# A two-layer decoder step on one core: rows of a retention head turned inside the next head's second projection, partial sums copied first, products for the new state two steps earlier

## The reference

```
proj = h @ w_ret_in                      # per head: q and k (256 + 256), v (512), g (512)
scores = (q_i @ k_i.T) * decay_mat       # chunks of 128 rows
o = scores @ v_i + (q_i * q_decay) @ s
s = chunk_decay * s + (k_i * k_decay).T @ v_i
y = layernorm(o) * gn * silu(g)          # rows of one head, 512 wide
x = x + gate * (y @ w_ret_out)
```

## Time and profile before

| what | value |
|---|---|
| median of 3 runs (lowest, highest) | 657.1 us (657.0 to 658.63) |
| the profiled execution, its own time | 656.73 us |
| its span, first to last instruction | 654.9 us |
| TensorE busy | 607.1 us (93% of the span) |
| VectorE, ScalarE, GpSimd busy | 363.6, 237.2, 214.5 us |
| TensorE's mean granted clock | 0.984 |
| the four heads, first projection of head 0 to the end of head 3 | about 37 to 297 us |
| moved by DMA | 190.30 MB |

### The profile page before, as it was taken

The page is one execution under the profiler, slowest core; times in us unless marked ns, Lnnn a source line. Parts: engine busy times, 40 slices in busy tenths (PEclk is TensorE's granted clock), DMA queues, the critical chain, the costliest instruction groups (busy, mean ns, idle before and its releaser), DMA issues. The chain is left out here.

```text
span 654.9 us, 11425 instructions
## 1 busy us (share of the span) xinstructions
PE 607.1 (93%) x4335; PEld 378.9 (58%) x4335; DVE 363.6 (56%) x726; ACT 237.2 (36%) x488; POOL 214.5 (33%) x242
## 2 busy tenths in 40 slices
PE   6899999899989998998999999999999988659996
PEld 5576656666666666743567746777644555434441
DVE  3343747375736583646544723445797964873822
ACT  4245244524442444223223625554044246231010
POOL 0060128012702270204283368999800012110000
PEclk9999999999999999998999999999999999788998
DMA  8996374897589658993995734544999999999982
GB/s 306 378 384 250 130 272 156 304 357 259 171 311 356 238 202 295 376 389 127 318 336 205 259 134 144 187 176 155 385 397 397 409 406 407 408 400 410 400 346 84
DMA packets 82370, 190.30 MB, mean 291 GB/s; under 512 B 4167, under 2 KB 12631, under 8 KB 82316
## 3 DMA queue, kind: packets, MB, share of 16 engines
q1 hardware_dynamic: 80484, 183.71, 75.5%
q0 software_dynamic: 1296, 4.46, 2.4%
q10 hardware_dynamic: 536, 1.41, 0.6%
HBM read 167.14 MB, written 22.41 MB: 289 GB/s over the span
## 5 line engine op out<-in xcount | busy, mean ns | idle before, releaser
L553 POOL TENSOR_TENSOR weights_low<-ring,weights_high 128x512 fp32r<-128x512 f32 x96 | 124.0, 1332 | 74.3 <-PE bank L800 39.9
L1391 ACT ACTIVATE weights_high<-ring 128x1024 fp32r<-128x1024 f32 x84 | 86.6, 1054 | 101.1 <-PE bank L819 55.7
L811 PE MATMUL bank<-weights_high,h_high 128*128 128x512 f32 x272 | 109.2, 402 | 0.0
L811 PE MATMUL bank<-weights_high,h_low 128*128 128x512 f32 x272 | 107.1, 394 | 0.0
L819 PE MATMUL bank<-weights_low,h_high 128*128 128x512 f32 x272 | 83.9, 404 | 4.7 <-DVE weights_low L553 4.5
L811 PEld LDWEIGHTS bank<-weights_high,h_high 128*128 128x128 f32 x272 | 51.0, 188 | 25.5 <-issue 14.2
L819 PEld LDWEIGHTS bank<-weights_low,h_high 128*128 128x128 f32 x272 | 48.9, 188 | 20.8 <-DVE weights_low L553 7.5
L811 PEld LDWEIGHTS bank<-weights_high,h_low 128*128 128x128 f32 x272 | 51.2, 188 | 11.0
L553 DVE TENSOR_TENSOR weights_low<-ring,weights_high 128x512 fp32r<-128x512 f32 x72 | 44.7, 684 | 16.6 <-PE bank L710 11.4
L1975 DVE SCALAR_TENSOR_TENSOR ring<-ring,bank 128x512 f32<-128x512 f32 x64 | 41.8, 684 | 18.4 <-PE bank L994 14.9
L1915 DVE TENSOR_TENSOR partial_low<-bank,partial_high 128x512 fp32r<-128x512 f32 x26 | 17.8, 686 | 56.9 <-ACT partial_high L1342 31.0
(11 more groups left out here) (272 smaller groups left out, 1008.6 us busy)
## 6 DMA issues: line engine op xcount, KB each, us to landing
ring<-in_w_ada SPq DMA_DIRECT2D x12, 2048.0 KB, 13.4
ring<-in_cache_k SPq DMA_DIRECT2D x40, 512.0 KB, 8.6
ring<-in_cache_v SPq DMA_DIRECT2D x40, 512.0 KB, 9.9
ring<-in_w_ret_in SPq DMA_DIRECT2D x8, 2048.0 KB, 12.6
ring<-in_state_ret SPq DMA_DIRECT2D x32, 512.0 KB, 9.2
out_state_sample<-ring SPq DMA_DIRECT2D x32, 512.0 KB, 6.9
ring<-in_w_moba_in SPq DMA_DIRECT2D x8, 2048.0 KB, 8.9
arena<-in_cache_k SPq DMA_DIRECT2D x24, 512.0 KB, 10.8
```

Of the source, the lines that this page charges most:

```text
L553: tensor_tensor(w_low[:, slot, k, :], ring[:, slot, k * CH:(k + 1) * CH], high[:, k, :].bitcast(F32), ALU.subtract).then_inc(low_ready[LOW ...
L811: pe.matmul(o[i][:, :], xs[p][i][:, k, :], high[:, k, :], start=k == 0 and p == 0, stop=False)
L1391: nc.scalar.activation(w_high[u[0] == "moba"][:, 2 * i:2 * i + 2, :].rearrange("p a b -> p (a b)"), w[:, 2 * i * CH:(2 * i + 2) * CH], ACT ...
```

## The change

1. TensorE: the new-state products of the head before are called at k = 0, 2, 4, 6 of unit 0 in place of 2, 4, 6, 8.
2. TensorE: the y tiles of the head before are turned one at a time at k = 2, 4, 6 of unit 1, no longer all three after it.
3. ScalarE: `copy_part` of unit 0 stands ahead of all roundings of unit 1's weights; `copy_part` of unit 1 stands ahead of all roundings of unit 2's weights (this holds in head 0 too); the copies of turned tiles 0 and 1 stand ahead of the first two of these roundings, that of tile 2 between the two pairs.

The rows of the last head are still turned after the loop, all three together. No instruction is added or left out, and no DMA.

```
-            def turn_y(h):
-                for n in range(3):
+            def turn_y(h, tiles=(0, 1, 2)):
+                for n in tiles:
                     pe.wait_ge(y_ready, 3 * h + n + 1)
                     turn(("yT", h, n), [L0["y"][:, n, k * P:(k + 1) * P] for k in range(4)])
...
-                if k in (2, 4, 6, 8):
-                    new_four(h - 1, k // 2 - 1)
+                if k < KT and k % 2 == 0:
+                    new_four(h - 1, k // 2)
+
+            def y_of_head_before(k):
+
+                if k in (2, 4, 6):
+                    turn_y(h - 1, (k // 2 - 1,))
...
-                project_parts(("ret", h, 1), ("ret", h, 1))
-                if h:
-                    turn_y(h - 1)
+                project_parts(("ret", h, 1), ("ret", h, 1), y_of_head_before if h else None)
...
-                high_weights(("ret", h, 1), range(2))
                 copy_part(("ret", h, 0))
-                high_weights(("ret", h, 1), range(2, 4))
+                high_weights(("ret", h, 1), range(4))
...
+                copy_part(("ret", h, 1))
+
+                def y_turned(tiles):
+                    if h:
+                        for n in tiles:
+                            turned(L0["yT"][:, 4 * h - 4:4 * h, :], ("yT", h - 1, n), n)
+
+                y_turned((0, 1))
                 high_weights(("ret", h, 2), range(2))
-                copy_part(("ret", h, 1))
+                y_turned((2,))
                 high_weights(("ret", h, 2), range(2, 4))
-                if h:
-                    for n in range(3):
-                        turned(L0["yT"][:, 4 * h - 4:4 * h, :], ("yT", h - 1, n), n)
```

## The result

| | before | changed |
|---|---|---|
| median (lowest, highest), 4 runs each | 657.51 us (657.0 to 658.63) | 650.58 us (649.46 to 651.73) |
| ratio of the two, 95% interval | | 0.9892 [0.9867, 0.9918] |
| profiled execution, its span | 654.9 us | 648.0 us |
| TensorE's mean granted clock | 0.984 | 0.984 |

The changed kernel is 1.1% faster. The forecast was 650.4 us, a gain of 6.7; the measured gain is 6.9, and its interval goes from 5.4 to 8.7.

The account below looks back on a forecast made before the run. The prediction took TensorE, working 93% of the span, as the bound. Terms 6.2 + 1.65 - 1.1 = 6.7 us took the profiled 656.73 us to 650.0; the median, 0.37 above, gave 650.4 us, range 648.2 to 654.2.

Parts of the forecast that it names:

- What TensorE gains in the heads reaches the end: TensorE's gain in the heads should move layer 1's cache stage and the end; 1.3 us either way behind the heads.
- the sum: Gains of 6.2 and 1.65 us in units 1, less 1.1 us lost in units 0: 6.7 us.
- Partial sums copied first: Unit 1, all four heads: copying ahead of the roundings removes TensorE's wait for weight slice 6, 6.2 us gained.
- rival (d): Unit 1: slice 6 waits for something other than ScalarE's copy; 656.6 us, chance 0.04.
- Turned rows inside: Heads 1 to 3: transposes of y inside unit 1 shorten the section behind it; 0.55 us a head, 1.65 us gained.
- rival (c): Unit 1: transposes between matmuls don't overlap, each takes some 0.28 us, costing 6.1 us; 656.5 us, chance 0.03.
- Products two steps earlier: Unit 0, heads 1 to 3: waits for banks of 0.9 us in place of 0.55; some 1.1 us lost.
- The earlier writes and loads: In each head SyncE writes states and issues weight and modulation loads about 2 us earlier; no gain counted.
- rival (a): Head 3: DMAs don't come forward with TensorE; third modulation load follows its slot, 1.8 us return as wait; 652.2 us, chance 0.12.
- a sign of being wrong: Head 3 waiting for modulation weights or states by more than 0.2 us was one of those listed.
- Rival (b), the clock: After new short waits or at late stops the granted clock goes wrong: 1.3 to 3 us lost; 652.5 us, chance 0.09.
- Rival (e), the products tie TensorE to VectorE: Unit 0: every product set waits for VectorE's reads, over 4 us lost a head; 660.7 us at 3.4 more; chance 0.04.

Follow-up runs that it names:

- e1: The kernel before with only ScalarE's two copies of partial sums put first, ahead of the weight roundings: 652.03 us, ratio 0.9911.
- e3: The changed kernel with the new-state products back at k = 2, 4, 6, 8: 650.28 us, ratio 0.9878 to the kernel before.
- e2: The changed kernel with the partial-sum copies behind two roundings again and the products back in their place, leaving only the turns moved: 652.28 us, ratio 0.9912.
- e5: The changed kernel itself, run again beside other variants on one chip: 650.16 us, ratio 0.9891 to the kernel before.
- e6: The changed kernel with VectorE's two prompt-state copies ahead of the third layer norm in heads 0 to 2: 650.58 us, ratio 0.9886.
- e8: e3 with half of each odd new state of head 2 left unwritten, so that output is incomplete: 648.98 us, ratio 0.9861.
- e10: The changed kernel itself, run again in the last group of runs: 650.57 us, ratio 0.9893 to the kernel before.
- e11: The changed kernel with products at k = 1, 3, 5, 7 and VectorE's prompt-state copies ahead of the third layer norm: 649.79 us, ratio 0.9886.
- e9: The changed kernel with the new-state products at k = 1, 3, 5, 7: 649.02 us, ratio 0.9874 to the kernel before.

## Why the prediction held, step by step

- *What TensorE gains in the heads reaches the end.* 6.24 us in the heads' record, 6.9 in the span and in the medians. Right. That the medians meet the forecast to 0.2 us is luck: the heads gave 0.5 us less than the sum, and the rest of the 6.9 lies in stretches that vary by more than that in recordings of one kernel. In the changed kernel units 1 with their turns gave 8.0 us where the sum has 7.85, units 0 took 1.97 where it has 1.1, and head 3's rest gave 0.19.
- *Partial sums copied first, 6.2 us.* Alone it gave 0.63 us in head 0 and 1.94, 2.00, 1.52 in the others, 6.1 us in units 1 (e1). Right, and rival (d) with it out.
- *Turned rows inside, 1.65 us.* The changed kernel's stages with late products (e3) are 0.70 us shorter than e1's, 2.1 us for three: 0.45 us better than the sum. The section behind the unit takes 2.04 us in them and not head 0's 2.10, as its wait for VectorE is 0.44 us and not 0.51, and the three sets add 1.24 us (1.29 in the changed kernel) and not 1.32. A set costs 0.44 us in its step (117.94 to 118.30, and the low pair behind it 0.1 longer), as the earlier trace rows said, which puts rival (c) out. By the figure of about 275 ns for one transpose in the Trainium skill (TensorE: Matmul & The Clock Gate, PE-mode transpose) a set would have cost 1.1 us; the trace has that figure as the length of one record (0.27 us), not as what each one costs. What the sum didn't say is that this part alone is worth 4.6 us (e2), since its cost is then hidden in the wait. The sum was right only because it took this wait away first.
- *Products two steps earlier, 1.1 us lost.* Here a term was mis-sized. The first set's wait is 0.85 us, as worked out; but the third was to wait "hardly", and it waits 0.32 us: VectorE begins its second four only 0.65 us after it could, having stood for TensorE's set (102.66), and then takes the slow 3.19 us. So a unit 0 loses 0.60 to 0.69 us and not 0.37, 1.97 in all.
- *The earlier writes and loads.* The prediction moved them by 2 us and gave that no value. In head 3 they have one. Once one or both of the other parts are in, TensorE waits 1.0 to 1.7 us for states with late or odd products, and 0 to 0.6 with early ones (0.6 in e5 and e6, over the 0.2 that the prediction named as a sign of being wrong). That is the wait of rival (a), which the change itself keeps small, but not by the path that rival (a) gave. The third modulation load didn't hang on its slot: with the full write all three were issued together as soon as the last write had landed, a wait of 10.4 us in the changed kernel. Only with half the write (e8) did the third wait for its slot, 1.6 us. The earlier products give back 1.1 to 1.7 of the 1.97 us. The net cost of moving the products is thus 0.3 to 0.8 us, beside the 1.1 predicted. Two errors met, the waits put too low and the earlier loads put at nothing.
- *Rival (b), the clock.* The stop after head 3 stayed at 3.1 us in each recording; the sixteen matmuls behind it took 3.19 us before, 2.55 in the changed kernel, and between 1.92 (e5, e10, e11) and 3.64 (e9) in the others. It follows the granted clock and not the edit: in the first 6 us behind the stop the clock was 1.00 in e5, 0.72 in the changed kernel's first recording, 0.78 before and 0.50 in e9. From line 710 to the first unit of layer 1 it takes 92.7 us in the three recordings in which the clock didn't fall there, 93.9 to 94.3 in nine others and 95.5 in e9. It is scatter of the size that was put down, and in the changed kernel's first recording the clock was 1.00 all through the heads, the new short waits included.
- *Rival (e), the products tie TensorE to VectorE.* They do, in two sets of four, at 1.2 us a head where the sum had 0.9; far from the 3.4 more that were needed.

## What to carry to other kernels

Work placed in a wait cost nothing here, but it and the removal of the wait then gain in part the same microseconds: decide which wait is left once all edits are in, and price each part against that. When a producer is moved earlier, ask which bank its first write needs and who reads that bank last; one step later the first set waited for nothing here, at the price of later writes of the states. An instruction that copies a small result should not stand behind one that waits for a DMA, unless it needs it; and when TensorE gains time, look for the place where the DMA queue has no slack (here head 3), since part of the gain stays there.

## What the runs showed of the hardware

- A 3.1 us stop of TensorE was followed by sixteen equal matmuls in anything from 1.92 to 3.64 us, in programs that differ little or (e5, e10 and the first recording of the changed kernel) not at all. The granted clock behind the stop fell from 2.4 to 1.2 GHz for a while in ten of the thirteen recordings and didn't in three. In the kernel before it was 0.58 from 300 to 303 us, partly at either level; in e9 it was 0.50, all at 1.2 GHz, over the 6 us in which the matmuls took longest. The fall cost 1.3 to 1.6 us in nine of them and 2.8 in e9, by the distance from line 710 to the first unit of layer 1.
- The shorter stops in the heads didn't do this. After the 0.85 us that the first set waits, one matmul takes 0.34 us to the next start, and from there on they follow at their 0.23 us (starts at 100.42, 100.65, 100.88). Three of them in the changed kernel's first recording:

```profile
100.42 0.39 PE L811 MATMUL bank<-weights_high,h_low 128*128 128x512 f32 x1
100.65 0.39 PE L811 MATMUL bank<-weights_high,h_high 128*128 128x512 f32 x1
100.88 0.40 PE L811 MATMUL bank<-weights_high,h_low 128*128 128x512 f32 x1
```

- A matmul stream that stops loses 0.4 us more than the idle time that the profile names, in all four heads of the kernel before: in head 1 the last six low matmuls took 3.36 us with 1.56 us of idle, where 1.39 would do. Some 0.17 us of it is only how the records lie, 0.40 us long at a distance of 0.23; the other 0.24 us is the slower start of the first four behind the stop, 126.31 to 127.48 where 0.93 would do.
- A 128 x 128 float32 transpose has a record of 0.27 us, but eight in a row take 1.03 us, and a set of four among matmuls adds 0.44 us, 0.11 us for each.
